# The last matrix of a feed-forward layer, from fp32 products to three passes of rounded parts

## The reference, cut to what matters

```python
D_FF_DENSE = 2816
def swiglu(x, w1, w3, w2):
    return (jax.nn.silu(x @ w1) * (x @ w3)) @ w2
# in second_block, layer 0:
    ffn = swiglu(x, ffn_w1[i], ffn_w3[i], ffn_w2[i])
    x = layer_norm_2(DEEPNORM_ALPHA * x + ffn, ln2_g[layer], ln2_b[layer])
```

## Time and profile before

| | us |
|---|---|
| median of three runs | 2485.46 |
| lowest and highest | 2479.89, 2486.88 |
| the profiled execution, whole | 2485.01 |
| its span | 2483.2 |
| `ffn1` and `ffn3` on TensorE, from the third slot of `ffn1` | 115.2 |
| `ffn2` on TensorE, up to the sum of line 724 | 70.7 |
| from there to the first product of layer 1 | 23.4 |

### The profile page before, as it was taken

One profiled execution on the slowest core, in us unless ns is written; L12 is line 12 of the kernel. 1 busy time (PEld: TensorE's weight loads), 2 busy tenths in 40 slices (PEclk: granted clock), 3 DMA queues, 4 the chain that ended last, 5 costly groups with the idle time before them and its releaser, 6 DMA issues.

```text
span 2483.2 us, 35228 instructions
## 1 busy us (share of the span) xinstructions
PE 2345.2 (94%) x13506; PEld 1495.7 (60%) x13507; DVE 722.3 (29%) x1358; ACT 589.0 (24%) x867; POOL 299.4 (12%) x131
## 2 busy tenths in 40 slices
PE   5999899999999999999988999999899989999997
PEld 4877754444444444444448887999798875445444
DVE  6744322222222222222252334100313341111113
ACT  1033111211111111112134741430267010111111
POOL 1000000000000000000014522580265000000000
PEclk8999889999999999999998998999999979999999
DMA  9952479999999999989973423553543257799751
GB/s 371 369 199 88 102 285 418 418 418 418 417 418 417 418 417 418 418 343 417 417 285 114 122 81 102 187 187 103 169 150 105 108 224 279 306 407 401 280 227 69
DMA packets 226471, 688.60 MB, mean 277 GB/s; under 512 B 31386, under 2 KB 120418, under 8 KB 190562
## 3 DMA queue, kind: packets, MB, share of 16 engines
q1 hardware_dynamic: 221776, 685.82, 72.0%
q10 hardware_dynamic: 4626, 1.81, 0.3%
HBM read 686.53 MB, written 1.05 MB: 277 GB/s over the span
## 4 chain that ended last, share of the span: by engine, by line
PE 73%; DMA 10%; SPq 8%; DVE 4%; issue 1%; ACT 1%; ACTq 1%; DVEq 0%
PE PS L958 16%; PE PS L635 12%; PE PS L646 11%; DMA RAW<-in_w_exp_in 9%; PE PS L1054 7%; SPq L439 6%; PE PS L1065 4%; PE PS L922 4%; PE PS L1237 3%; PE PS L941 2%; PE PS L1018 2%; PE PS L690 1%; PE PS L667 1%; PE PS L732 1%; PE PS L969 1%
## 5 line engine op out<-in xcount | busy, mean ns | idle before, releaser
L958 PE MATMUL PS<-RAW,Z 128*64 128x512 f32 x3168 | 715.5, 599 | 24.2 <-DMA RAW<-in_w_exp_in 23.2
L958 PEld LDWEIGHTS PS<-RAW,Z 128*64 128x64 f32 x3168 | 214.4, 137 | 456.6 <-issue 379.2
L387 POOL TENSOR_TENSOR WLO_D<-W,WHI_D 128x2048 fp32r<-128x2048 f32 x60 | 275.9, 4602 | 1305.2 <-ACT WHI_D L384 1305.2
L1054 PE MATMUL PS<-W,Z 128*64 128x384 f32 (+1 forms) x1408 | 216.3, 464 | 8.8 <-DMA W<-in_moe_w 5.5
L1054 PEld LDWEIGHTS PS<-W,Z 128*64 128x64 f32 x1408 | 100.2, 138 | 126.3 <-issue 70.3
L646 PE MATMUL PS<-Z,W 128*128 128x256 f32 x768 | 173.2, 387 | 2.2 <-DVE Z L1828 1.5
L646 PEld LDWEIGHTS PS<-Z,W 128*128 128x128 f32 x768 | 148.7, 194 | 25.7 <-DVE Z L1828 1.9
L384 ACT ACTIVATE WHI_D<-W 128x2048 fp32r<-128x2048 f32 x60 | 114.4, 1906 | 167.4 <-DMA W<-in_w_in 92.6
L922 PE MATMUL PS<-Z 128*128 128x64 f32 x1088 | 128.6, 278 | 0.5 <-DVE Z L1933 0.5
L922 PEld LDWEIGHTS PS<-Z 128*128 128x128 f32 x1088 | 127.4, 196 | 0.9 <-issue 0.9
L646 PE MATMUL PS<-H,W 128*128 128x256 f32 x512 | 121.4, 400 | 2.9 <-ACT Z L1380 2.9
(11 more groups left out here) (377 smaller groups left out, 2395.3 us busy)
## 6 DMA issues: line engine op xcount, KB each, us to landing
RAW<-in_w_exp_in SPq DMA_DIRECT2D x256, 1024.0 KB, 19.2
RAW<-in_w_exp_out SPq DMA_DIRECT2D x128, 1024.0 KB, 21.7
W<-in_moe_w SPq DMA_DIRECT2D x128, 704.0 KB, 15.0
W<-in_w_in SPq DMA_DIRECT2D x52, 1024.0 KB, 6.3
W<-in_moe_w SPq DMA_DIRECT2D x40, 1024.0 KB, 14.3
W<-in_ffn_w SPq DMA_DIRECT2D x33, 1024.0 KB, 5.3
W<-in_w_ada SPq DMA_DIRECT2D x24, 1024.0 KB, 13.7
W<-in_w_out SPq DMA_DIRECT2D x12, 1024.0 KB, 5.0
```

The lines of the kernel that those rows point to most:

```text
L387: eng.tensor_tensor(lo, raw, hi.bitcast(F32), ALU.subtract).then_inc(sem("dense_lo"), 1)
L958: mm = pe.matmul(ps(bank, 512, 64 * h, 64 * h + 64), x, w[:, c:c + 512], start=first, stop=final, skip_group_check=True)
L1054: mm = pe.matmul(ps(2 * i + b, n, 64 * h, 64 * h + 64), X1[:, s, :], first2(s)[:, c:c + n], start=(s == 0), stop=(s == 7), skip_group_chec ...
```

## The change

`ffn2` becomes a split matrix. Its 11 slots enter the order of splits between those of `ffn3` and those of `qa1`, so the indexes of layer 1 move from 41 to 52. For each block and tile `down` issues three rounded passes in place of the fp32 product. Its inputs are split as well: VectorE writes the product of the two branches into half of `SQ` (`hidden_raw`, two places in turn), ACT rounds it into `FHI`, which lies over `Z`, and VectorE subtracts into `hidden_lo`, which lies over `H` and the rest of `Z`, one slot behind the multiplications. ACT splits one weight slot in each turn of that loop. Two of layer 1's first four slots, 54 and 55, are split after `final_x` instead of before the root's table.

```diff
-        self.split = ... or name in ("ffn1", "ffn3")
+        self.split = ... or name in ("ffn1", "ffn3", "ffn2")
...
+        def hidden_lo(s):
+            return FLO_H[:, 2 * s:2 * s + 2, :] if s < 4 else FLO[:, 2 * s - 8:2 * s - 6, :]
+
+        def hidden_raw(s):
+            return SQ[:, (s % 2) * 512:(s % 2 + 1) * 512].rearrange("p (k t) -> p k t", t=T)
...
-            for q in range(19, 41):
+            for q in range(19, 52):
                 split_dense(pool, q)
...
             def down(s, w, j):
-                for i in range(2):
-                    k = 2 * s + i
-                    mm = pe.matmul(ps(j // 2, T, c0=(j % 2) * T), w[:, i, j * P:(j + 1) * P],
-                                   Z[:, k * T:(k + 1) * T], start=(k == 0 and j % 2 == 0), stop=(k == 21),
-                                   skip_group_check=True)
+                hi, lo = FHI[:, 2 * s:2 * s + 2, :], hidden_lo(s)
+                for n, (a, x) in enumerate(((0, hi), (1, hi), (0, lo))):
+                    for i in range(2):
+                        mm = pe.matmul(ps(j // 2, T, c0=(j % 2) * T), w[a][:, i, j * P:(j + 1) * P], x[:, i, :],
+                                       start=(s == n == i == 0 and j % 2 == 0), stop=(s == 10 and n == 2 and i == 1),
+                                       skip_group_check=True)
                 return mm
             def hidden_ready(s):
-                e, c = job_evac[lins["ffn3"].job0 + s]
-                pe.wait_ge(sem("evac_" + e), max(c, job_evac[lin.job0 - 1][1] if s == 0 else 0))
-                return weights(lin.at[s]).rearrange("p (k n) -> p k n", k=2)
+                if s == 0:
+                    pe.wait_ge(sem("evac_dve"), job_evac[lin.job0 - 1][1])
+                pe.wait_ge(sem("ffn_lo"), s + 1)
+                q = split_ready(lin, s) % SPLIT_N
+                return [w[:, q, :].rearrange("p (k n) -> p k n", k=2) for w in (WHI_D, WLO_D)]
...
-            for q in range(19 + SPLIT_N + 11, 41 + SPLIT_N):
+            for s in range(11):
+                split_dense(act, 30 + SPLIT_N + s)
+                act.wait_ge(sem("evac_dve"), job_evac[lins["ffn3"].job0 + s][1])
+                act.activation(FHI[:, 2 * s:2 * s + 2, :], hidden_raw(s), ACT.Copy).then_inc(sem("ffn_hi"), 1)
+            for q in range(41 + SPLIT_N, 54):
                 split_dense(act, q)
             root_table()
             norm_root()
             final_x(3, V_LN2G, V_LN2B)
+            for q in range(54, 56):
+                split_dense(act, q)
             mixer2(1)
...
+            def hidden_split(s):
+                dve.wait_ge(sem("ffn_hi"), s + 1)
+                dve.tensor_tensor(hidden_lo(s), hidden_raw(s), FHI[:, 2 * s:2 * s + 2, :].bitcast(F32), ALU.subtract).then_inc(sem("ffn_lo"), 1)
             for s in range(11):
                 b = linear_ready(lins["ffn3"], s)
-                o = z(2 * s, 2 * s + 2)
-                dve.tensor_tensor(o, ps2(b), o, ALU.mult).then_inc(sem("evac_dve"), 1)
+                if s >= 2:
+                    dve.wait_ge(sem("ffn_lo"), s - 1)
+                dve.tensor_tensor(hidden_raw(s), ps2(b), z(2 * s, 2 * s + 2), ALU.mult).then_inc(sem("evac_dve"), 1)
+                if s:
+                    hidden_split(s - 1)
+            hidden_split(10)
```

More of the change, by code:

```diff
@@ L65, in __init__ @@
         self.is_ada = name.startswith("ada")
-        self.split = name.rstrip("01") in ("qa", "kva", "ret", "gg") or name in ("ffn1", "ffn3")
+        self.split = name.rstrip("01") in ("qa", "kva", "ret", "gg") or name in ("ffn1", "ffn3", "ffn2")
 def plan():
@@ L170, in build_two_blocks @@
         W1_2 = sb("W1_2", [P, w_bytes])
+        with nc.sbuf_tensor("FHI", [P, 22, T], F32R) as FHI, nc.sbuf_tensor("FLO", [P, 16, T], F32R) as FLO:
+            pass
         Z = sb("Z", [P, 38 * T])
         X = sb("X", [P, KT, T])
+        with nc.sbuf_tensor("FLO_H", [P, KT, T], F32R) as FLO_H:
+            pass
         H = sb("H", [P, KT, T])
@@ L563, in mixer2 @@
             def mixer2(l):
-                q0 = 41 * l
+                q0 = 52 * l
                 for q in range(q0, q0 + 11):
@@ L1513, in copy @@
                     act.activation(dst, ps2(b), f).then_inc(sem("evac_act"), 1)
-                q0 = 41 * l + SPLIT_N
+                q0 = 52 * l + SPLIT_N
                 for s in range(2):
```

## The result

| | before | changed |
|---|---|---|
| median, us | 2485.46 | 2465.61 |
| lowest and highest of 5 | 2479.89, 2488.88 | 2465.14, 2469.71 |
| the profiled execution | 2485.01 | 2468.71 |
| its span | 2483.2 | 2466.9 |

The ratio is 0.9928, with a 95% interval of 0.9915 to 0.9940: the kernel is faster by 0.6 to 0.85%, about 20 us by the medians, where 16 were forecast. The two profiled executions are 16.3 us apart.

What follows compares the result with a forecast made beforehand. The prediction took the stretch as bound by TensorE's matmul throughput, then by VectorE's norm chain. Matmuls -12.0, collisions -5.2, clock -0.5 and late third slot +1.6 gave -16.1 us, 2469 us, range 2461 to 2478.

Steps and rivals of the forecast that it cites:

- The price of a pass: In the last feed-forward matrix a pass costs 0.120 us, three 0.360 against 0.433 in fp32; 164 products save 12.0 us.
- rival B: A pass costs a quarter of an fp32 product, 0.108 us, saving another 5.8 us, 2463; chance 0.06.
- The ring: In the last matrix four slot places keep weight splits ahead of TensorE: no cost, 6.8 us per slot if uncovered.
- Rival C: In the last matrix the slot places starve, holes slow the clock, passes cost 0.213 us: 46 us more, 2515; chance 0.04.
- The collisions: At the layer norm, two VectorE instructions stretched beside POOL's splits return to 0.69 us, gaining 5.2 us.
- the clock: Half-speed sums behind the TensorE hole at the norm run at full clock, gaining 0.5 us.
- Rival A: At the norm, POOL's split of slot 53 comes later and stretches a VectorE instruction again: 2475; chance 0.12.
- The giving back: In layer 1's mixer the third slot is ready 15.8 us after the first activation; TensorE's stall costs 1.6 us.
- rival D: In layer 1's mixer slots 55 and 56 are late, giving back 8 us or more, 2478 to 2482; chance 0.06.
- The last 12 lie under VectorE: At the end of the last matrix, 12 of 176 products are off the chain, so only 164 count.
- The size: Whole profiled execution: -12.0 - 5.2 - 0.5 + 1.6 = -16.1 us, from 2485.0 to 2469.

Runs made afterwards that it cites:

- experiment 4: The changed kernel with two passes (low weights by high inputs left out): 2450.89 us, one run; with a fourth pass (low weights by low inputs): 2485.69 us.
- experiment 1: The kernel before, fp32 kept, with only splits 43 and 44 moved behind the new stream's activations: 2480.13 us against 2485.87, ratio 0.9978.
- experiment 2: The changed kernel with splits 54 and 55 put back ahead of the norm: 2478.0 us; with only 54 put back: 2473.7 us in a single run.

## Why the prediction was right, point by point

- The price of a pass. 0.120 us was forecast from the block ahead, 0.1205 was measured with other operands and another order, and rival B (0.108) is out. Three passes are worth 0.36 against 0.433. The page "FP8 and Floating Point Precision" of the Trainium skill (section "TensorE Precision Notes") has four passes for true fp32. By that count and the 0.433 us measured, three would cost 0.325, an estimate that the trace does not bear out: four rounded passes take 0.48 us here (experiment 4), more than the fp32 product, and no profile here shows less than 0.120 for a single one with 256 columns.
- The ring. No hole in the last matrix, as forecast, and with two passes the hole came where the same sum puts it (3.7 us for 3.8). Rival C did not come about.
- The collisions. Both went. Alone, in experiment 1, they are worth 5.2 us up to the statistics, where the prediction has 5.2 and 0.5 for the clock. That they come from POOL is shown by moving its splits: away from the norm in experiment 1 the stretched instructions take 0.69 us, put back in experiment 2 others are stretched. The prediction read the rows a little wrong: the two instructions end not with POOL's subtraction but 0.55 us behind it (1769.45 against 1768.90, 1778.58 against 1778.04). The page "SBUF — State Buffer" (Trainium skill, section "SBUF: two separate sides") has an exclusive lock between a VectorE instruction with two SBUF inputs and a GpSimd one that reads SBUF. By it the traces agree: such instructions of 0.69 us that start beside a subtraction of POOL take up to 5.06 us, those that read PSUM keep their 0.69 beside it.
- Rival A, with a margin of 1.9 us, did not come about; the margin was 1.92. It took one collision for a loss of 5.7 us. Experiment 2 shows 2.9 us for one collision and 11.3 for two, so it was priced too high for one and far too low for two.
- The giving back. The third slot began 15.6 us after the first activation of line 1356 (15.8 forecast), and TensorE waited 0.96 us for it. The prediction has a stall of 1.6 us with short first products at half clock and 0.5 with long ones, and they were between. Slots 55 and later were not late, and rival D did not come about.
- The step that failed in detail: "The last 12 lie under VectorE". In the changed kernel they don't, as experiment 4 shows (176 products count). Against experiment 1, which has the same tail, the passes bring 12.6 us up to the statistics and not 12.0, and the collisions with the clock 5.2 and not 5.7. The sum of both, 17.7 forecast and 17.8 measured, came out by the balance of the two, and because the prediction also followed TensorE to its end of slot 10 (70.7 forecast, 70.56 measured).
- The size. The sum for the profiled execution was -16.1 us, the stretch gave 16.2 and the spans differ by 16.3. That the spans fit so well is in part luck: what lies ahead of the stretch and behind it is off by 3 us each and cancels. Against the medians the forecast of 2469 was 3.4 us too high, within its range. Two terms were sized from one profile of before that is at the cheap end: the collisions (1.4 us more in two others) and the 1.6 us given back. From the first line of the statistics to the third slot the changed kernel takes 1.6 us more than the profile shown of before, but only 0.6 and 0.7 more than the two others.

## What to carry to other kernels

Price a matmul by the distance of the same form of instruction in the block beside it; three rounded passes beat fp32 here by 0.073 us a product, and four lose. Before moving work to POOL, look at which VectorE instructions with two SBUF operands will run beside it, above all in a norm, where one can wait for a whole POOL instruction (4.6 us here) and leave TensorE a hole with a slow clock behind it: two splits in the wrong place cost 11.3 us here. And where a collision or a clock step is in the part that changes, take more than one profile of the kernel before.

## What the runs showed of the hardware that I had not expected

- Two collisions of VectorE with POOL cost more than twice one: 11.3 us against 2.9. Behind the hole of 4.01 us on TensorE the granted clock was 0.50 for 5 us; behind one of 2.09 it was 0.57 over 4 us.
- VectorE subtracts 128x2048 fp32 elements from SBUF in 2.29 us, POOL in 4.62.
- The first products of layer 1 run at half clock for a varying length: 64 passes took 9.27 to 10.56 us in these profiles, with 4.86 to 5.21 us of idle time ahead of them, and the longest and the shortest both had 5.21.
